# Attention jobs in a two-block transformer kernel: the values matmuls of a job behind the transposes of the next one, and VectorE's weights ahead of the next scores

## What is computed

```python
# first block, each of its 2 layers: 8 heads of 64, keys chosen by an indexer
logits = einsum('bqgrd,bqkgd->bqgrk', qg, kg) * scale      # queries in blocks of 128
p = softmax(where(valid, logits, -inf)); o = einsum('bqgrk,bqkgd->bqgrd', p, vg)
# second block, layer 0 (beside a gated delta rule): 4 heads of 128, causal
p = softmax(where(kpos <= qpos, q @ k.T * scale, -inf)); o = p @ v
# second block, layer 1: 8 heads, two products in each score
scores = q_nope @ k_nope.T + q_rope @ k_rope.T
o = softmax(where(kpos <= qpos, scores, -inf)) @ val
```

## Time and profile before

| | |
|---|---|
| median of 3 runs | 4166.0 us (4164.74 to 4166.89) |
| time of the profiled execution | 4166.68 us |
| its span, first to last instruction | 4164.9 us |
| PE busy, share of the span | 3981.3 us, 96% |
| DVE busy | 2086.6 us, 50% |
| ACT busy | 1469.7 us, 35% |
| mean granted clock of PE | 0.973 |

### The profile page before, as it was taken

The page is one execution under the profiler, slowest core; times in us unless marked ns, Lnnn a source line. Parts: engine busy times, 40 slices in busy tenths (PEclk is TensorE's granted clock), DMA queues, the critical chain, the costliest instruction groups (busy, mean ns, idle before and its releaser), DMA issues.

```text
span 4164.9 us, 67253 instructions
## 1 busy us (share of the span) xinstructions
PE 3981.3 (96%) x24777; PEld 3559.0 (85%) x24777; DVE 2086.6 (50%) x4729; ACT 1469.7 (35%) x3011; POOL 346.3 (8%) x470
## 2 busy tenths in 40 slices
PE   8999999999999999999999999999989999999999
PEld 6977889978788898797888889888868889889888
DVE  1434335423253354622398555555432995555555
ACT  2222126311221273211234444444432344444444
POOL 4001100040011000000017000000000080000000
PEclk9998999999999999999999999999999999999999
DMA  5562245554522465446342445454433424454453
GB/s 139 139 174 59 61 117 162 163 130 124 152 59 64 116 176 146 115 122 181 110 119 89 170 174 170 169 173 168 138 88 108 140 65 174 169 175 170 169 174 122
DMA packets 652839, 565.64 MB, mean 136 GB/s; under 512 B 56523, under 2 KB 585946, under 8 KB 652250
## 3 DMA queue, kind: packets, MB, share of 16 engines
q1 hardware_dynamic: 652004, 559.59, 44.7%
q0 software_dynamic: 352, 3.15, 0.2%
q10 hardware_dynamic: 278, 0.08, 0.0%
HBM read 553.30 MB, written 9.44 MB: 135 GB/s over the span
## 4 chain that ended last, share of the span: by engine, by line
PE 92%; DVE 4%; ACT 2%; issue 1%; SPq 0%; DMA 0%; DVEq 0%; ACTq 0%
PE bank L734 22%; PE bank L1173 13%; PE bank L754 9%; PE bank L1187 6%; PE bank L1188 6%; PE bank L1186 6%; PE bank L1125 5%; PE bank L823 4%; PE bank L1162 4%; PE bank L1140 3%; PE bank L730 2%; PE bank L1115 1%; PE bank L919 1%; PE bank L929 1%; PE bank L917 1%
## 5 line engine op out<-in xcount | busy, mean ns | idle before, releaser
L734 PE MATMUL bank<-hT,ring 128*128 128x256 f32 (+1 forms) x3184 | 722.2, 387 | 23.2 <-ACT hT L1405 16.2
L734 PEld LDWEIGHTS bank<-hT,ring 128*128 128x128 f32 (+1 forms) x3184 | 608.7, 192 | 121.4 <-issue 31.7
L1173 PE MATMUL bank<-h_high,u_parts 128*128 128x256 f32 x3072 | 437.8, 285 | 0.0
L2625 DVE TENSOR_TENSOR u_parts<-bank,u_parts 128x512 fp32r<-128x512 f32 x384 | 247.4, 686 | 327.3 <-ACT u_parts L1696 327.3
L1186 PE MATMUL bank<-v_high,w_low 128*128 128x512 f32 x1024 | 406.6, 397 | 0.4 <-DVE v_low L2646 0.4
L1187 PE MATMUL bank<-v_low,w_high 128*128 128x512 f32 x1024 | 406.0, 396 | 0.0
L1188 PE MATMUL bank<-v_high,w_high 128*128 128x512 f32 x1024 | 404.9, 395 | 0.0
L1173 PEld LDWEIGHTS bank<-h_high,u_parts 128*128 128x128 f32 x3072 | 395.5, 189 | 5.9
L1395 ACT ACTIVATE arena<-bank 128x256 f32<-128x256 f32 (+2 forms) x326 | 124.8, 386 | 697.9 <-PE bank L734 530.0
L2646 DVE TENSOR_TENSOR v_low<-ring,v_high 128x512 fp32r<-128x512 f32 x512 | 337.1, 690 | 65.9 <-ACT v_high L1713 41.8
L1696 ACT ACTIVATE u_parts<-bank 128x512 fp32r<-128x512 f32 x384 | 207.4, 591 | 351.8 <-PE bank L1173 346.2
(11 more groups left out here) (393 smaller groups left out, 6036.4 us busy)
## 6 DMA issues: line engine op xcount, KB each, us to landing
ring<-in_peer_u SPq DMA_DIRECT2D x256, 512.0 KB, 4.1
ring<-in_peer_v SPq DMA_DIRECT2D x256, 512.0 KB, 3.5
ring<-in_w_in SPq DMA_DIRECT2D x132, 512.0 KB, 3.8
ring<-in_mod_w SPq DMA_DIRECT2D x96, 512.0 KB, 4.2
ring<-in_mlp_up SPq DMA_DIRECT2D x64, 512.0 KB, 4.0
ring<-in_mlp_down SPq DMA_DIRECT2D x64, 512.0 KB, 4.0
ring<-in_w_branch SPq DMA_DIRECT2D x64, 256.0 KB, 2.8
ring<-in_peer_w_q SPq DMA_DIRECT2D x32, 512.0 KB, 3.9
```

What stands on the lines that cost most here:

```text
L734: ins = eng.matmul(ps[0:n, 0:width], wv[:, i, :], moving(u * 8 + i), start=(u == 0 and i == 0), stop=(u == count - 1 and i == k - 1))
L1173: ins = eng.matmul(PB[6 + b][:, 0:S], u_parts[:, part, k * P:k * P + P], moving[:, k, :], start=(n == 0), stop=(n == len(products) - 1))
L2625: tt_(u_parts[:, 1, d], PB[4 + q][:, :], u_parts[:, 0, d].bitcast(F32), ALU.subtract).then_inc(sem("uL_ready"), 1)
```

## The change

On PE, `values(j)` is cut in two: `turned(j)` holds the wait for `p_ready` and the transposes, `values(j)` the wait for `pT_ready` and the matmuls. Iteration j issues `turned(j)` and then `values(j - 1)`; `values` of the last job stands behind the loop. On ACT `outputs(j)` is cut in the same way into `columns(j)` and `outputs(j)`, and iteration j issues `columns(j)` and then `outputs(j - 1)`. On DVE `weights(j)` now stands ahead of `scores(j + 1)` where it stood behind it. No instruction is added or removed, no buffer changes, and the fills stay where they are. Behind the edited place the lines of ACT and DVE move by 6 and 12 or more, and L880 becomes L883.

```diff
--- before.py
+++ after.py
@@ -865,7 +865,7 @@
                                          stop=(i == len(job["scores"]) - 1))
                     ins.then_inc(sem("score_mm"), 1)
 
-                def values(j):
+                def turned(j):
                     job, ps = jobs[j], PB[4 + j % 2]
                     eng.wait_ge(sem("p_ready"), pe.next("p_ready"))
                     if pe.reused("pv_out", 2):
@@ -873,6 +873,9 @@
                     for t in range(job["ns"] // P):
                         ins = eng.transpose(ps[:, t * P:t * P + P], probs[:, j % 2, t * P:t * P + P], C("ident"))
                     ins.then_inc(sem("pT_mm"), 1)
+
+                def values(j):
+                    job, ps = jobs[j], PB[4 + j % 2]
                     eng.wait_ge(sem("pT_ready"), pe.next("pT_ready"))
                     if "projected" in job:
                         eng.wait_ge(sem("evac"), tiles[job["projected"][1]][0] + 1)
@@ -887,7 +890,10 @@
                         scores(j + 1)
                     for label in fill[j] if fill else ():
                         project(label)
-                    values(j)
+                    turned(j)
+                    if j:
+                        values(j - 1)
+                values(len(jobs) - 1)
                 eng.wait_ge(sem("pv_out"), pe.uses["pv_out"])
 
             def group_norm(y, fill=()):
@@ -1447,13 +1453,16 @@
                     eng.activation(probs[:, j % 2, 0:ns], probs[:, j % 2, 0:ns], ACT.Exp, bias=nmx[:, j % 2:j % 2 + 1],
                                    accum_out=den[:, j % 2:j % 2 + 1]).then_inc(sem("exp_ready"), 1)
 
-                def outputs(j):
+                def columns(j):
                     job = jobs[j]
                     eng.wait_ge(sem("pT_mm"), act.next("pT_mm"))
                     if act.reused("pv_mm", 2):
                         eng.wait_ge(sem("pv_mm"), act.freed("pv_mm", 2))
                     eng.activation(probsT[:, j % 2, 0:job["ns"]], PB[4 + j % 2][:, 0:job["ns"]],
                                    ACT.Copy).then_inc(sem("pT_ready"), 1)
+
+                def outputs(j):
+                    job = jobs[j]
                     eng.wait_ge(sem("pv_mm"), act.next("pv_mm"))
                     eng.activation(job["dest"], PB[4 + j % 2][job["rows"], 256:384],
                                    ACT.Copy).then_inc(sem("pv_out"), 1)
@@ -1464,7 +1473,10 @@
                         exps(j + 1)
                     for label in fill[j] if fill else ():
                         projected(label)
-                    outputs(j)
+                    columns(j)
+                    if j:
+                        outputs(j - 1)
+                outputs(len(jobs) - 1)
 
             def inverse(blocks, fill=iter(())):
                 for n in range(5):
@@ -2165,9 +2177,9 @@
 
                 scores(0)
                 for j in range(len(jobs)):
+                    weights(j)
                     if j + 1 < len(jobs):
                         scores(j + 1)
-                    weights(j)
 
             def group_norm(y, dst, eps):
```

## The result

The changed kernel takes 4118.7 us (median of 4 runs, 4115.3 to 4122.0) where the one before takes 4165.4 (4 runs, 4164.6 to 4166.9): the ratio is 0.9887, 95% interval 0.987 to 0.9905. So it is 46.7 us faster, where I had forecast 34.5 and a range that ended at 4121. The sign, the mechanism and the places were as forecast; the size was not. In two later comparisons the kernel before had medians of 4163.8 and 4164.0 and single times from 4156.3 to 4167.1, and the changed one a median of 4119.5, ratio 0.9893 (0.9877 to 0.991). The gain is thus better put at 44 to 47 us.

The account below looks back on a forecast made before the run. PE was taken to bound the kernel. The terms 9.6 + 11.8 + 8.2 + 4.5 + 0.8 - 0.4 = 34.5 us, off 4166.68 or 4166.0, gave 4132 us, with bounds 4123 to 4137 and a range of 4121 to 4141.

Parts of the forecast that it names:

- What bounds the kernel: PE, busy for 96% of the span and holding 92% of the chain; its idle time on its path is kernel time.
- The first term: PE's gap from transposes to values in all four attentions shrinks to 0.22 or 0.33 us, gaining 9.6, 11.8 and 8.2 us.
- The high end: Weight loads also go wholly under the preceding group: 42.7 us gained, 4123 us; one case in ten, inside the forecast's 85.
- The second term: Fourth attention: with DVE's weights ahead of the next scores, 7 waits of 0.64 us behind the short fill go, 4.5 us.
- The third term: Fourth attention's ends: 0.8 us gained at its end, 0.4 us lost at the scores of job 2; last softmax wait stays.
- The clock: Shifts of PE's low-clock fall behind the attention move the time by one or two us for each of two stretches.
- The loads into the ring: Rival, first two attentions: weight loads at 168 GB/s are the limit, 17 us less gain, 4149 us; 6 in 100.
- The serial chain of DVE: Rival: DVE's next scores wait for the exp, PE could stand in all 56 jobs; slower, for example 4188; 3 in 100.

Follow-up runs that it names:

- the experiment above: Against the changed kernel, PE issues the values of job j - 1 ahead of the transposes of job j; measured 4127.2 us (4 runs).
- the second profile of before: The kernel before, run and profiled once more with no edit: 4165.6 us (11 runs), ratio 1.0002; this profile's span is 4154.8 us.

## Why the prediction was wrong in size

**What bounds the kernel.** Right. PE holds 93% of the chain after, and what PE no longer waits went through to the end: nothing was given back later.

**The first term, what is left of the gap.** This is the step that failed. I took 0.10 to 0.11 us for passing from one group to the next from the row 3108.09 to 3108.41, where two values entries (0.22 us) take 0.32. But those values had themselves just waited for the copy; the row says so, 0.37. The same two entries in the fourth attention after, without a wait ahead of them, take 0.22 us in each of the 7 heads:

```profile
3027.00 0.30 PEld L883 LDWEIGHTS bank<-arena 128*128 128x128 f32 x2
...
3027.11 0.39 PE L883 MATMUL bank<-arena 128*128 128x128 f32 x2
...
3027.33 1.03 PE L864 MATMUL bank<-arena 128*128 128x256 f32 x4
```

So in that row the 0.10 came with the stall, and I counted as a cost that would remain at the new passage one that would go at the old. The weight loads show what such rows have in common. Before, the first load of L880 starts with its matmul, both held by the wait:

```profile
255.67 0.30 PEld L880 LDWEIGHTS bank<-arena 128*128 128x128 f32 x2 [0.56 <-ACT arena L1455]
```

After, the load of the values starts at 257.62, together with the transposes, and their matmul at 257.78:

```profile
257.62 0.14 PEld L874 LDWEIGHTS bank<-cst,arena 128*128 128x128 f32 x1 [0.19 <-issue]
...
257.62 0.36 PEld L883 LDWEIGHTS bank<-arena 128*128 128x128 f32 x2
```

A wait is not the only thing that puts a load beside its matmul. The scores of the first attention, with their 64 rows, have it there too (258.10 and 258.10), and the values ahead of them still take 0.32 us with no wait; and with the values right behind the fill of 48 columns (the experiment above) it is so again:

```profile
260.73 0.30 PEld L883 LDWEIGHTS bank<-arena 128*128 128x128 f32 x2 [0.18 <-issue]
260.73 0.49 PE L883 MATMUL bank<-arena 128*128 128x128 f32 x2
...
261.06 0.27 PE L874 MATMUL bank<-cst,arena 128*128 128x128 f32 x1
```

In all of these rows of two matmul entries a first load that starts beside its matmul, the group's own or the next one's, goes with about 0.10 us more, and loads that start 0.11 us ahead go with none. Something is given back, too: in the fourth attention the values of two key tiles and the scores behind them take 0.62 and 0.52 us after, where they took 0.55 and 0.45 before, and there the scores' load starts only 0.03 us ahead. That the load is the cause is read from this agreement; no run tests it alone.

In the first three attentions the error enters twice, 0.06 us at the transposes and 0.09 to 0.10 at the values: 0.15 us a job, 6.0 us over their 40 jobs. There 21.4 us had been forecast, and 26.3 were measured with the third taken against the second profile of before (the last job of each still stalls, so not all 6.0 could come). In the fourth 13.1 had been forecast and 15.4 came. There the two distances from transposes to values fell from 1.72 us a head to 0.33, by 1.39 and not 1.17: 0.22 us a head.

The high end of the range was to be the case of the rule of the Trainium skill (TensorE: Matmul & The Clock Gate, "Step-by-step: what each phase is for") that PE pulls a weight load ahead of matmuls in flight. The trace after agrees at the values, with the load at 257.62, and not at the scores of the first attention, 258.10. The high end, 42.7 us, was nearly the 40.6 to 42.9 that the attentions gave, and I had put it at one case in ten.

**The second term, DVE's order.** The 7 waits of 0.64 us went, as said, but were worth 0.86 each, 6.0 us and not 4.5. Here the error is another one. The first term was worked out from start to start, this one from the idle time in the profile. The transposes behind the short fill, after:

```profile
3026.00 1.06 PE L730 MATMUL bank<-ring,arena 128*128 128x128 f32 x8
...
3026.89 0.38 PE L874 MATMUL bank<-cst,arena 128*128 128x128 f32 x2
```

From the start of L730 to the transposes it is 0.89 us where it was 1.70: 0.81 gained and not 0.64. The fill's last entry ends at 3027.06, and transposes that nothing holds start 0.17 us before that; idle time is counted only from its end. The remaining 0.05 us are in the row behind the wait (0.28 from the transposes to the values with the wait, 0.22 without). So the errors of the two terms in the fourth attention are 0.22 and 0.17 us a head, less some 0.05 given back in the other rows: 7 times 0.34, about the 2.3 us that came beyond the forecast there. That the gain of this part depends on the other I had not seen; taken alone it moves the wait to the copy.

**The third term, the ends.** Right: 5.52 for 5.55 us at the end, a wait of 0.46 us for the evacuation at the scores of job 2 for the 0.4, and the first job's wait stays.

**The clock.** I allowed one or two us for each of two stretches. The trace of one kernel moves by 10 us of span between two executions with the mean granted clock (0.973 and 0.976), and by 6.3 us ahead of the first attention alone. Behind the first attention the fall is nearly as it was, 0.55 over 18 us where it was 0.57. The profile that I worked from was one of the slower ones. Of the 46.7 us, 40.6 to 42.9 are shown in the attentions. What the other 2 to 6 are is not shown. They are well within what moves by itself: outside the attentions the ten profiles of this document add up to between 3893 and 3906 us, and both of these are profiles of the kernel before; the three of the whole change have 3895 to 3897. But the later medians keep 44.5, and the mean granted clock over all executions hardly differs, 0.975 in 39 of before and 0.974 in 8 of after. So the record doesn't show that PE stands less at the lower level on average with the change, and the remainder stays open.

**The rivals.** The loads into the ring never became the limit (196 GB/s where I had asked about 168). The serial chain of DVE costs nothing where a fill lies between two jobs, and 0.7 us in the one place where I made two jobs meet. With both terms right the sum would have been 34.5 + 4.9 + 2.3 = 41.7 us, which is 4124; the result at 4118.7 would still have needed a range that holds the clock's 5 us to each side.

## What to carry to other kernels

A stall of TensorE costs more than its idle time in the profile: here also 0.17 us by which the next entry would have started before the last one's end, and 0.05 to 0.10 us in the row behind the wait, where the weight load starts beside its matmul. So take what a wait costs from start to start, and to price what remains when it is removed, take a row whose own group did not wait and whose neighbours are those of the new order. When a wait is taken from one link of a chain over three engines, look at which signal ends last next; here DVE's new order alone gave half of what it gave with the other two engines one stage further ahead. And before a difference of some us is explained, profile the unchanged kernel twice.

## What was not expected of the hardware

The same kernel ran from 4156.3 to 4167.1 us, with the mean granted clock of PE in step with it: of 39 executions of the kernel before the six at 0.976 took 4156.3 to 4157.1 us, and the five at 0.973 took 4166.2 to 4167.1. A wait on PE that is already met costs next to nothing (18 more wait instructions of 51 ns in 64 us: 0.1 us). Between two rows of PE the same two matmul entries take 0.22 us or 0.32 to 0.33, by whether the first weight load of their group, or of the next one, starts ahead of its matmul or beside it; a wait is one cause of the second, a fill of 48 columns ahead another.
